# Reciprocal softmax sums turned by one transpose ahead of the value products, in the mixing attention of a four-block model

## The reference

```python
def attend(q, k, v):                     # context and grouped-query heads
    s = jnp.einsum('bqkgd,bskd->bkgqs', q, k) * q.shape[-1] ** -0.5
    p = jax.nn.softmax(s.astype(jnp.float32), axis=-1).astype(v.dtype)
    return jnp.einsum('bkgqs,bskd->bqkgd', p, v)

def neighbourhood_attention(...):        # local heads, per grid row
    s = jnp.concatenate([s_loc + bias, s_ctx], axis=-1)
    p = jax.nn.softmax(s.astype(jnp.float32), axis=-1)
    return p_loc @ v_win + p_ctx @ v_ctx
```

## Time and profile before

| | us |
|---|---|
| median of 3 runs | 3201.33 |
| lowest and highest of them | 3199.23, 3203.04 |
| the profiled execution | 3203.01 |
| its span in the trace | 3201.0 |
| TensorE busy | 3098.1 (97%) |
| VectorE busy | 1889.2 (59%) |
| ScalarE busy | 1358.3 (42%) |
| mixing attention of layer 0, in the trace | about 1665 to 1842 |
| mixing attention of layer 1, in the trace | about 2640 to 2757 |

### The profile page before, as it was taken

How to read it: one execution, slowest core, us unless ns; L and a number is a source line. 1 busy time by engine, 2 the same in 40 slices (tenths; PEclk the granted TensorE clock), 3 DMA queues, 4 the chain that set the end, 5 groups by cost and what they waited for, 6 DMA issues and landing times.

```text
span 3201.0 us, 49513 instructions
## 1 busy us (share of the span) xinstructions
PE 3098.1 (97%) x20714; PEld 2617.1 (82%) x20714; DVE 1889.2 (59%) x3148; ACT 1358.3 (42%) x2487; POOL 804.4 (25%) x866
## 2 busy tenths in 40 slices
PE   7999999999999999999999999999998999999999
PEld 5787889997887889897876687899997777778997
DVE  6646477667433586675237646866564427567664
ACT  6556433445434533443235533422322336433443
POOL 1302132443110213441011106123322411013441
PEclk9999999999999999999999999999999999999999
DMA  4111132322327233222325421212211303022231
GB/s 140 54 54 54 41 104 81 113 85 96 105 79 272 98 107 103 94 79 80 87 102 195 125 87 53 70 50 80 80 56 37 107 21 99 27 79 93 82 116 40
DMA packets 191022, 282.08 MB, mean 88 GB/s; under 512 B 19400, under 2 KB 122440, under 8 KB 190672
## 3 DMA queue, kind: packets, MB, share of 16 engines
q1 hardware_dynamic: 188912, 273.24, 25.7%
q10 hardware_dynamic: 1888, 5.69, 0.5%
HBM read 273.66 MB, written 2.10 MB: 86 GB/s over the span
## 4 chain that ended last, share of the span: by engine, by line
PE 89%; DVE 4%; ACT 3%; POOL 2%; issue 1%; DMA 1%; ACTq 0%; DVEq 0%; POOLq 0%; SPq 0%
PE ps L549 6%; PE ps L550 6%; PE ps L551 6%; PE ps L1013 5%; PE ps L1015 5%; PE ps L1014 5%; PE ps L1046 4%; PE ps L1047 3%; PE ps L1048 3%; PE ps L443 3%; PE ps L1478 2%; PE ps L1476 2%; PE ps L1477 2%; PE ps L2524 2%; PE ps L635 2%; PE ps L634 2%
## 5 line engine op out<-in xcount | busy, mean ns | idle before, releaser
L452 ACT ACTIVATE R<-ring 128x512 fp32r<-128x512 f32 (+2 forms) x485 | 438.2, 912 | 378.3 <-PE ps L1510 107.5
L549 PE MATMUL ps<-R,R 128*128 128x512 f32 (+1 forms) x1016 | 396.7, 390 | 15.4 <-DVE ringlo L655 4.6
L1013 PE MATMUL ps<-R,R 128*128 128x256 f32 x1344 | 381.3, 284 | 3.4 <-ACT U L452 3.4
L1014 PE MATMUL ps<-R,R 128*128 128x256 f32 x1344 | 381.0, 283 | 0.0
L550 PE MATMUL ps<-R,R 128*128 128x512 f32 (+1 forms) x1016 | 380.1, 374 | 0.0
L551 PE MATMUL ps<-R,ringlo 128*128 128x512 f32 (+1 forms) x1016 | 379.5, 373 | 0.0
L452 ACT ACTIVATE U<-ps 128x512 f32<-128x512 f32 (+6 forms) x370 | 182.2, 508 | 458.5 <-PE ps L1015 171.8
L655 DVE TENSOR_TENSOR ringlo<-ring,R 128x1024 fp32r<-128x1024 f32 (+1 forms) x141 | 173.0, 1234 | 251.4 <-ACT R L452 251.2
L452 ACT ACTIVATE R<-U 128x512 fp32r<-128x512 f32 (+2 forms) x283 | 179.2, 641 | 250.5 <-POOL U L1146 84.3
L1013 PEld LDWEIGHTS ps<-R,R 128*128 128x128 f32 x1344 | 258.3, 192 | 7.9 <-ACT U L452 3.8
L1014 PEld LDWEIGHTS ps<-R,R 128*128 128x128 f32 x1344 | 258.4, 192 | 3.4
(11 more groups left out here) (416 smaller groups left out, 7376.3 us busy)
## 6 DMA issues: line engine op xcount, KB each, us to landing
ring<-in_w_mod SPq DMA_DIRECT2D x24, 2048.0 KB, 9.6
ring<-in_ffn_w_in SPq DMA_DIRECT2D x44, 1024.0 KB, 7.7
ring<-in_w_ffn_in SPq DMA_DIRECT2D x44, 1024.0 KB, 7.8
ring<-in_ffn_w_out SPq DMA_DIRECT2D x18, 1024.0 KB, 8.8
ring<-in_dil_w_in SPq DMA_DIRECT2D x9, 2048.0 KB, 7.9
ring<-in_w_ffn_out SPq DMA_DIRECT2D x18, 1024.0 KB, 9.7
ring<-in_gdn_w_in SPq DMA_DIRECT2D x8, 2048.0 KB, 8.9
ring<-in_w_in SPq DMA_DIRECT2D x6, 1536.0 KB, 6.9
```

Source lines behind the costliest of these rows:

```text
L452: return act.e.activation(o, i, fn, **kw)
L549: pe.e.matmul(ps[:, 0:x.n], hi[:, k, :], x.hi[k], start=(k == 0), stop=False)
L1013: pe.e.matmul(ps, hi[:, k, :], share(h, 0)[:, k, :], start=(first and k == 0), stop=False, skip_group_check=go_on)
L1014: pe.e.matmul(ps, hi[:, k, :], share(h, 1)[:, k, :], start=False, stop=False, skip_group_check=go_on)
```

## The change

ScalarE gets a new instruction for each step, `act_rden`. In iteration n it waits for the reciprocals of step n-3 and for the transpose that read the last such tile, and copies the two columns of reciprocals, broadcast to 64 columns each, into a tile of 128x128. It stands behind the side work and ahead of the copies and of the exponentials. There are two tiles, one for narrow and one for wide steps. TensorE waits for this tile as soon as it has the value bank, turns it with one transpose into `ps[:, 128:256]`, and then makes the value products; the two products behind them and their wait are gone, and the last value product now gives the semaphore `value`.

The rest makes room. The scratch tile is gone, and the squares go into the gating branch's own input half. `pool_split_keys` of layer 0 waits for the last of these squares, and `pool_norm_weights` waits for the last transpose of a narrow tile.

```diff
         def pe_values(tag, m):
             ps = bank(tag, m, "value")
+            pe.wait_ge(*at("rden tile", tag, m))
+            tp([(ps[:, 128:256], MIX["rden"][step_wide(tag, m)])]).then_inc(*pe.done("rden turned", tag, m))
             for c in step_chunks(tag, m):
                 pe.wait_ge(*at("p", tag, m, c))
...
-                    pe.e.matmul(ps[64 * e:64 * e + 64, 0:128], job.values[i], P[:, o:o + 128], start=(i == 0),
-                                stop=(i == n - 1))
-            pe.wait_ge(*at("rden", tag, m))
-            for e in range(2):
-                t = pe.e.matmul(ps[64 * e:64 * e + 64, 128:256], stats(m, e)[:, 3:4].broadcast_to([128, 64]), ident,
-                                start=True, stop=True)
+                    t = pe.e.matmul(ps[64 * e:64 * e + 64, 0:128], job.values[i], P[:, o:o + 128], start=(i == 0),
+                                    stop=(i == n - 1))
             t.then_inc(*pe.done("value", tag, m))
...
+        def act_rden(tag, m):
+            act.wait_ge(*at("rden", tag, m))
+            if m:
+                act.wait_ge(*at("rden turned", tag, m - 1))
+            tile = MIX["rden"][step_wide(tag, m)]
+            activate(tile.rearrange("p (e x) -> p e x", e=2), both_stats(m, 3).unsqueeze(2).broadcast_to([128, 2, 64]),
+                     ACT.Copy).then_inc(*act.done("rden tile", tag, m))
...
                 side(n)
                 chunks = list(step_chunks(tag, n - 2)) if 0 <= n - 2 < n_steps else []
                 late = n >= first_wide(tag)
+                if n >= 3:
+                    act_rden(tag, n - 3)
                 if late:
...
-        STS, SG, SCR = take(6, 24), take(24), take(256)
+        STS, SG = take(6, 24), take(24)
+        MIX["rden"] = [U[:, o:o + 128] for o in (4096 + o2[0], 31552)]
...
         def pool_split_keys(l):
             if l == 0:
-                pool.wait_ge(*at("gate out", l, len(mix_outs(l)) - 1, 3))
+                pool.wait_ge(*at("group sum", l, len(mix_outs(l)) - 1))
...
-            activate(SCR, OTS[s][:, t, :], ACT.Square, accum_out=SG[:, i:i + 1]).then_inc(*act.done("group sum", l, i))
+            activate(gate_tiles(l, i)[2], OTS[s][:, t, :], ACT.Square, accum_out=SG[:, i:i + 1]).then_inc(*act.done("group sum", l, i))
...
                     pool.wait_ge(*at("group rstd", l))
+                    pool.wait_ge(*at("rden turned", ("mix", l), first_wide(("mix", l)) - 1))
                     pool_norm_weights(N_POST[l], P_O)
```

## The result

| | before | after |
|---|---|---|
| median, us | 3200.28 (4 runs) | 3226.43 (4 runs) |
| lowest and highest | 3195.41, 3203.04 | 3221.22, 3236.53 |
| ratio after / before | | 1.0082, 95% interval 1.0068 to 1.0096 |
| profiled execution | 3203.01 | 3236.53 |
| its span, and mean granted clock | 3201.0, 0.991 | 3234.5, 0.986 |

The kernel is 26 us (0.8%) slower. A second series of four runs of the kernel after, beside its own runs of before, gave 3226.73 against 3203.08, ratio 1.0080 (1.0066 to 1.0095).

What follows compares the result with a forecast made beforehand. TensorE, busy 97% of the span, was taken as the bound. Layer 0 wide steps 8.7, its boundary 3.0, layer 1 10.5, narrow steps -3.1 gave +19.1 us on 3201.3: 3220 us, range 3206 to 3232.

Steps and rivals of the forecast that it cites:

- the loop reciprocal, tile, copy of chunk 0, values, scores, maxima, reciprocal: Wide steps: copy of chunk 0 queues behind tile and reciprocal, delaying values and the next reciprocal; 3220 us, chance 0.70.
- a term of 1.16: Wide steps: values start 1.16 us after the reciprocal, from 0.03 + 0.28 (tile) + 0.60 (copy) + 0.05 + 0.2 (transpose, gap).
- TensorE's saving: Each step: one transpose of 0.11 us replaces two products of 0.22 us, saving 0.11 us, 6.6 us over 60 steps.
- cover: Narrow steps: reciprocal ends 3.5 us before its values, so the tile arrives in time; 31 steps keep their gain, -3.1 us.
- The slip of 0.88 - d: Each wide step starts its values later by 1.16 - 0.28 - d us; 0.88 lies between 0.7 and 1.05.
- d: Wide steps before the change: start of the values less end of the reciprocal, such as -0.17 or +0.13 us.
- the sum: Slips added over wide steps: 8.0 us for layer 0's steps 24 to 34, 10.1 for layer 1's 9 to 22.
- a rival with 0.06: TensorE's clock falls in all 26 wide iterations, costing 52 us beyond the 19: 3272 us, chance 0.06.
- A PEclk below 1.00 in the wide windows: Named sign that the forecast is wrong: TensorE's granted clock below 1.00 in the wide steps.
- The boundary: Layer 0, steps 20 to 24: values now wait for the reciprocal with its tile or copy; growth of 3.5 us.
- 3209: Rival: the wide-step loop holds only partly, with half of the slip, +8 us; chance 0.12.
- 3195: Rival: the new wait is hidden and TensorE's saving of 6.6 us remains; chance 0.12.

Runs made afterwards that it cites:

- the second execution: Kernel after, unchanged, run and profiled again: span 3225.3 us, median 3226.73 us against 3203.08 of before.
- The wait alone: Kernel before plus one ScalarE wait for the reciprocal of step n-3, without tile or transpose: 3221.58 us against 3202.05 of before.
- the tile twice: Kernel after with ScalarE copying each tile twice, the second behind the first: 3242.11 us against 3202.46 of before.
- the waits were filled with three products: Kernel after plus three fp32 128x128 constant products ahead of the value bank's wait in each wide iteration: 3226.94 us against 3202.46 of before.
- the early reciprocal: Kernel after with VectorE's late reciprocal moved ahead of its side work and maxima from first_wide on: 3199.49 us against 3202.05 of before.
- with nine: Kernel after plus nine fp32 128x128 constant products ahead of the value bank's wait in each wide iteration: 3248.01 us against 3203.08 of before.

## Why the prediction was right, and where its sizes were off

**The bound and the way.** Right: the loop reciprocal, tile, copy of chunk 0, values, scores, maxima, reciprocal. The values stand 1.14 us behind the reciprocal in all of steps 23 to 34 of layer 0 in the second execution, for a term of 1.16, and 0.72 behind it at step 35, which has no copy. Its parts were mixed: the tile holds the queue for 0.21 us (1794.04 to 1794.25) and not 0.28, and from the transpose to the values 0.26 pass and not 0.2. The period of step 27 is 5.61 us (1795.14 to 1800.75 by the values' starts), predicted 5.6. ScalarE's 60 tiles took 0.306 us each, for 0.31. The wait alone and the tile twice moved this distance to 0.68 and 1.48.

**TensorE's saving.** Right, 0.11 us a narrow step, cover included; only step 20 of layer 0 lost its gain (+0.21). Here the trace agrees with the Trainium skill (Perfetto Trace Analysis, "Transposes"): as an instruction the transpose is the better one, by 0.11 us. That the change as a whole is slower contradicts nothing in it; the section does not weigh who makes the operand.

**The slip of 0.88 - d.** Right to 0.04 a step: 8.4 us over ten wide steps of layer 0 where the sum gave 8.0. Every step there slips by 0.92 - d. The two errors are small and of opposite sign: 1.14 for 1.16, and the removed products shorten the loop by 0.22 and not 0.28, for the scores follow the values after 1.46 us (1795.14 to 1796.60) where I had put 1.40. In layer 1 it was 14.1 where the sum gave 10.1. The mis-sized term is the clock, which the sum left at nothing and gave to a rival with 0.06; only the upper end of the range was left open for a few falls. A PEclk below 1.00 in the wide windows was also named as a sign of being wrong, and layer 1 shows 0.94: that sign was too strict, since the loop holds in both layers and the falls only add to it. The three steps at the falls slipped by 1.0, 0.9 and 1.7 us more than 0.88 - d, 3.6 of the 4.0. The rival had the mechanism, but its price of 2 us in all 26 iterations was far off: it happens at a few fixed places, at 1 to 2 us. The prediction held 1.15 us of wait against it, which had left the clock at 1.00; one such wait leaves it there, a row of them does not always. What the Trainium skill says there (TensorE: Matmul & The Clock Gate, "A second HAM failure mode: psum-queue depth-cycling"), of a bf16 kernel, fits these fp32 wide steps better than I gave it credit for: three falls in layer 1, and one when the waits were filled with three products.

**The boundary.** 3.7 us instead of 3.5 from step 20 to 24. By the starts of the values it is spread otherwise than I wrote, 3.0 at steps 21 and 22 and 0.7 at steps 23 and 24: the values of 22 and 23 used to start ahead of their reciprocal and wait behind themselves, and I had counted from their ends.

**The range.** 3226 lies in it, 6 us above the forecast: of the 5.3 us between 19.1 and the 24.4 that the second execution shows in the attention, 3.6 are the clock in layer 1, 1.1 the slip and the boundary, 0.5 the last step of either layer and 0.1 the narrow steps. The rest, up to the 26 of the first series (23.7 in the second), lies within the spread of the runs. The rivals of 3209 and 3195 did not occur, and even the early reciprocal reached only 3199. Two readings of the prediction were off without moving its sum: two steps have d above 0.88 (13 and 19 of layer 1; step 22 has 0.86), not three, and the ends given for the tile and the gap put the 0.88 between about 0.6 and 1.0, not 0.7 and 1.05.

## What to carry to other kernels

When work moves to an engine that is idle a third of the time, ask what its first wait is for and which instruction of that queue somebody needs soonest: here a copy that TensorE waited for came to stand behind a result which arrived a microsecond later, and one bare wait gave three quarters of the loss. The test is cheap to read off a timeline: compare, step by step, the end of the new instruction's input with the end of the first old instruction that it now holds up. Before dropping such a change, move its input's producer earlier; that took back all 26 us here, though no more than the same move gives without the change.

## What the runs showed of the hardware

- A reciprocal on VectorE takes 0.16 us for 128x2 and 0.94 us for 128x128 float32: (942 - 156) / 126 = 6.2 ns for each further column, against 0.29 us for a copy or a product of 128x128 (L2643, L2646).
- A full fp32 128x128 product is two instructions and takes 0.22 us of TensorE (18 instructions in 2.0 us), one transpose of the same size 0.11. The two products of 64 columns each that the change removed are four instructions, and cost 0.22 together, 0.055 each: in the trace they start in pairs, 0.01 us apart within a pair and 0.11 us from pair to pair, so that the two products ran side by side.
- With waits of about a microsecond in nearly every wide iteration, TensorE's granted clock fell to the 1.2 GHz level at the same three steps of layer 1 (12, 15 and 22) in both profiled executions, and at the same three with the wait alone. With three products in the waits two of the three falls went away, with nine all three. One fall of the early reciprocal followed a single wait of 1.39 us; waits of 1.15 us in before brought none.
- From the end of one ScalarE instruction to TensorE's start took 0.05 us behind a 128x512 copy (1794.83 to 1794.88) and 0.14 us behind a 128x128 one (1787.83 to 1787.97). No run shows why they differ.
